# Two transformer blocks on one core: the feed-forward up-projection with high and low activations in one matmul

## The reference

```python
def conv_glu_ffn(h, w_up, conv_w, conv_b, w_down):
    S = h.shape[1]
    u = h @ w_up                       # 256 x 2048 @ 2048 x 11264
    up = jnp.pad(u, ((0, 0), (CONV_WIDTH - 1, 0), (0, 0)))
    u = sum(conv_w[j] * up[:, j:j + S] for j in range(CONV_WIDTH)) + conv_b
    val, gate = jnp.split(u, 2, axis=-1)
    return (jax.nn.silu(gate) * val) @ w_down
```

## Time and profile before

| | |
|---|---|
| median of 3 runs | 2526.63 us (2525.19 to 2527.48) |
| span of the profiled execution | 2525.9 us |
| HBM traffic | 611.66 MB, mean 242 GB/s |
| first up-projection | about 636 to 1124 us of the span |
| second up-projection | about 1760 to 2264 us |
| down-projections | about 1124 to 1370 and 2264 to 2500 us |

### The profile page before, as it was taken

The page is one execution under the profiler, slowest core; times in us unless marked ns, Lnnn a source line. Parts: engine busy times, 40 slices in busy tenths (PEclk is TensorE's granted clock), DMA queues, the critical chain, the costliest instruction groups (busy, mean ns, idle before and its releaser), DMA issues.

```text
span 2525.9 us, 50139 instructions
## 1 busy us (share of the span) xinstructions
PE 2484.3 (98%) x19624; PEld 2273.1 (90%) x19624; DVE 1440.5 (57%) x2436; ACT 1124.3 (45%) x1324; POOL 1232.5 (49%) x500
## 2 busy tenths in 40 slices
PE   7999999999999999999999999999999999999997
PEld 5897998899999999998887877899999999998886
DVE  2536666266767767776665633265766756453433
ACT  2253334434444444454444444344544444454443
POOL 2674445675444444454443666465444444444442
PEclk8999999999999999999999999999999999999998
DMA  9974565596777777777776565386666675556553
GB/s 399 397 271 178 200 234 201 224 385 221 276 286 265 267 274 281 267 260 275 272 272 243 182 258 207 130 313 254 220 233 222 216 258 184 184 180 200 192 191 117
DMA packets 140381, 611.66 MB, mean 242 GB/s; under 512 B 15584, under 2 KB 15968, under 8 KB 115680
## 3 DMA queue, kind: packets, MB, share of 16 engines
q1 hardware_dynamic: 140256, 609.88, 66.4%
HBM read 607.72 MB, written 2.10 MB: 241 GB/s over the span
## 4 chain that ended last, share of the span: by engine, by line
issue 45%; PE 33%; POOL 21%; POOLq 1%; DVE 0%; DMA 0%; ACT 0%; DVEq 0%; SPq 0%
PE psum L1971 33%; POOL wlo L1780 21%; POOLq L1777 0%; DMA ada_raw<-adastream 0%; DVE xT L2314 0%; POOLq L1779 0%; PE psum L2204 0%; DVE psum L2314 0%; ACT arena L1794 0%; POOLq L1780 0%; ACT arena L1791 0%; DVE arena L2429 0%; DVE acc L2306 0%; DVE acc L2314 0%; DVEq L388 0%
## 5 line engine op out<-in xcount | busy, mean ns | idle before, releaser
L1780 POOL TENSOR_TENSOR wlo<-raw,whi 128x1024 fp32r<-128x1024 f32 x496 | 1232.3, 2491 | 1264.2 <-ACT whi L1791 1263.2
L1791 ACT ACTIVATE whi<-raw 128x1024 fp32r<-128x1024 f32 x760 | 800.6, 1058 | 950.1 <-PE psum L1971 716.2
L1971 PE MATMUL psum<-hi_h,whi 128*128 128x256 f32 x4224 | 1206.4, 286 | 4.6 <-DVE lo_h L2314 2.3
L1971 PE MATMUL psum<-lo_h,whi 128*128 128x256 f32 x4224 | 1190.3, 282 | 0.0
L1971 PE MATMUL psum<-hi_h,wlo 128*128 128x256 f32 x4224 | 1190.2, 282 | 0.0
L1971 PEld LDWEIGHTS psum<-hi_h,whi 128*128 128x128 f32 x4224 | 798.4, 189 | 18.7 <-issue 8.5
L1971 PEld LDWEIGHTS psum<-hi_h,wlo 128*128 128x128 f32 x4224 | 798.8, 189 | 1.7 <-issue 1.4
L1971 PEld LDWEIGHTS psum<-lo_h,whi 128*128 128x128 f32 x4224 | 798.4, 189 | 0.0
L2306 DVE TENSOR_TENSOR wlo<-raw,whi 128x1024 fp32r<-128x1024 f32 x264 | 385.1, 1463 | 268.3 <-ACT whi L1791 268.3
L2314 DVE SCALAR_TENSOR_TENSOR psum<-ada_raw,cact,psum 128x256 f32<-128x256 f32 x814 | 342.4, 483 | 24.5 <-DMA ada_raw<-adastream 21.1
L1971 PE MATMUL psum<-whi,gshi 128*128 128x512 f32 x704 | 276.0, 392 | 0.3 <-DVE wlo L2306 0.3
(11 more groups left out here) (166 smaller groups left out, 1608.8 us busy)
## 6 DMA issues: line engine op xcount, KB each, us to landing
raw<-wstream SPq DMA_DIRECT2D x760, 512.0 KB, 4.6
ada_raw<-adastream SPq DMA_DIRECT2D x168, 1024.0 KB, 6.8
arena<-adastream SPq DMA_DIRECT2D x24, 1024.0 KB, 18.0
xT<-x_in SPq DMA_DIRECT2D x8, 512.0 KB, 7.1
y_out<-xT SPq DMA_DIRECT2D x4, 512.0 KB, 2.6
gs_pages<-tabs_in SPq DMA_DIRECT2D x2, 512.0 KB, 4.2
gs_pages<-rw_in SPq DMA_DIRECT2D x2, 512.0 KB, 6.7
tabs<-tabs_in SPq DMA_DIRECT2D x1, 482.0 KB, 8.5
```

Of the source, the lines that this page charges most:

```text
L1780: nc.gpsimd.tensor_tensor(wlo[:, q, :], raw[:, q, :], whi[:, q, :].bitcast(F32), ALU.subtract).then_inc(sem.lo_ready, 1)
L1791: return nc.scalar.activation(out_, in_, ACT.Copy, scale=scale)
L1971: return nc.tensor.matmul(o, lhsT, rhs, start=start, stop=stop, skip_group_check=True)
```

## The change

Where the high weights of a block meet the high and the low activations, the two matmuls of 256 columns become one of 512 columns.

- h is kept in one tensor `h_parts` in which the high and the low part of each row tile lie side by side (512 columns), so that one matmul can read both.
- In the up-projection (`slab_up`) 4 of 4 column tiles of the value half and 2 of 4 of the gate half (`WIDE`) have a PSUM bank each: the left 256 columns take high by high and low weight by high activation, the right 256 columns high weight by low activation. The value half now uses banks 0 to 3, the gate half banks 4 and 5, and its other two tiles share bank 6 with three matmuls as before.
- Behind a half ScalarE copies the right halves of the banks to the arena (`low_taken`), makes the high split of one slab, and waits for `whole`. VectorE, when its running modulation unit is through, waits for `low_taken` and adds the copy to the left halves in PSUM (`whole`). Then the taps follow as before. The high split of slab 11 of a turn comes ahead of the value half's tap (it stood behind it), that of slab 3 of the next turn ahead of the gate half's tap.
- TensorE's first half of an up-projection waits for both older pairs of banks; the first pieces of the down-projection wait for `free_val` alone.
- Some semaphores are shared (`f_exp` with `f_ln`, `gn_var` with `gn_mean`, `conv_landed` with `cols_landed`).

```diff
+WIDE = (4, 2)
-        hi_h, _ = sb("hi_h", [P, KT * S + 128], F32R)
-        lo_h, _ = sb("lo_h", [P, KT * S + 128], F32R)
-        hhi, mhi = (hi_h[:, a:a + KT * S].rearrange("p (k s) -> p k s", s=S) for a in (0, 32))
-        hlo, mlo = (lo_h[:, a:a + KT * S].rearrange("p (k s) -> p k s", s=S) for a in (0, 32))
+        h_parts, _ = sb("h_parts", [P, 2 * KT * S + 128], F32R)
+        hx, mx = (h_parts[:, a:a + 2 * KT * S].rearrange("p (k c s) -> p k c s", c=2, s=S) for a in (0, 32))
+        hhi, mhi = hx[:, :, 0, :], mx[:, :, 0, :]
+        hlo, mlo = hx[:, :, 1, :], mx[:, :, 1, :]
...
+        def up_place(half, j):
+
+            if half == 0 or j < 2:
+                return bank[4 * half + j][:, 0:S]
+            return bank[6][:, (j - 2) * S:(j - 1) * S]
+
+        def up_sums(half, low):
+            b = 4 * half
+            return psum[:, b:b + WIDE[half], low * S:(low + 1) * S]
...
-                        a, z = n1 + half * GS + 3 + (half == 0), n1 + half * GS + 3 + GS
+                        a, z = n1 + half * GS + 4, n1 + half * GS + 3 + GS
...
-                        u = pair(1 - half)
+                        copy(tiles(11 + half)[:, 0:WIDE[half], :], up_sums(half, 1)).then_inc(sem.low_taken, 1)
+                        if i is None:
+                            his(z, z + 1)
+                        else:
+                            hi(z, more, i)
+                        act.wait_ge(sem.whole, 2 * (gb + t + step) + half + 1)
                         for j in range(4):
                             c = 16 * half + 4 * j
-                            ins = fn(tiles(11 + half)[:, j, :], u[:, j, :], ACT.Identity,
+                            ins = fn(tiles(11 + half)[:, j, :], up_place(half, j), ACT.Identity,
                                      scale=cw[:, c:c + 1], bias=cw[:, c + 3:c + 4])
                             if j == 3:
                                 ins.then_inc(sem.gate_tap if half else sem.val_tap, 1)
-                    if i is None:
-                        his(n1 + more + 3, n1 + more + 4)
-                    else:
-                        hi(n1 + more + 3, more, i)
...
+            def slab_up(n, half, k, per=0, i=0):
+
+                ready(n, per, i)
+                q = n % RING
+                first, last = k == 0, k == GS - 1
+                for kk in range(2):
+                    kt = 2 * k + kk
+                    for j in range(4):
+                        w = slice(kk * 512 + j * P, kk * 512 + (j + 1) * P)
+                        if j < WIDE[half]:
+                            b = bank[4 * half + j]
+                            mm(b[:, 0:S], wlo[:, q, w], mhi[:, kt, :], first and kk == 0, False)
+                            ins = mm(b, whi[:, q, w], mx[:, kt, :, :].rearrange("p c s -> p (c s)"), False, last and kk == 1)
+                        else:
+                            ins = product(up_place(half, j), whi[:, q, w], wlo[:, q, w], mhi[:, kt, :], mlo[:, kt, :],
+                                          first and kk == 0 and j % 2 == 0, last and kk == 1)
+                        if kk == 1 and j == 3:
+                            ins.then_inc(sem.slab_used, 1)
...
                             quarter_unit(1, 1)
+                            dve.wait_ge(sem.low_taken, 2 * (NFF * b + done + i) + half + 1)
+                            tt(up_sums(half, 0), up_sums(half, 0), tiles(11 + half)[:, 0:WIDE[half], :],
+                               ALU.add).then_inc(*at.up(sem.whole))
 
                             dve.wait_ge((sem.val_tap, sem.gate_tap)[half], NFF * b + done + 1 + i)
```

More of the change, by code:

```diff
@@ L245, in __init__ @@
         self.sums_taken = new("sums_taken")
+        self.whole = new("whole")
         self.psum_zero = new("psum_zero")
@@ L268, in __init__ @@
         self.f_abs = new("f_abs")
-        self.f_exp = new("f_exp")
         self.f_ln = new("f_ln")
@@ L282, in __init__ @@
         self.gn_sd = new("gn_sd")
-        self.gn_var = new("gn_var")
         self.gs_hi = new("gs_hi")
@@ L305, in __init__ @@
         self.l2v = new("l2v")
+        self.low_taken = new("low_taken")
         self.lo2_ready = new("lo2_ready")
@@ L2155, in body @@
                     for half in range(2):
-                        p = 1 - half
                         free = (sem.free_val, sem.free_gate)[half]
                         if i is None and t == 0:
-                            pe.wait_ge(*st["free"][p])
+                            for p in range(2):
+                                pe.wait_ge(*st["free"][p])
                         else:
@@ L2166, in body @@
                                 pe.wait_ge(sem.h_ready, h0 + k + 1)
-                            slab(n0 + 2 * GS * t + half * GS + k, p, mhi[:, 2 * k:2 * k + 2, :],
-                                 mlo[:, 2 * k:2 * k + 2, :], k == 0, k == GS - 1, 2 * GS * per, 0 if i is None else i)
+                            slab_up(n0 + 2 * GS * t + half * GS + k, half, k, 2 * GS * per, 0 if i is None else i)
                         if units == 2:
@@ L2570, in ffn @@
                                 o, f = (slice(2, S), slice(0, S - 2)) if b == 0 else (slice(0, S - 1), slice(1, S))
-                                stt(t[:, j, o], u[:, j, f], cw[:, c + 2:c + 3], t[:, j, o], ALU.mult, ALU.add).then_inc(*at.up((sem.free_val, sem.free_gate)[half] if j == 3 else sem.step))
+                                stt(t[:, j, o], up_place(half, j)[:, f], cw[:, c + 2:c + 3], t[:, j, o], ALU.mult, ALU.add).then_inc(*at.up((sem.free_val, sem.free_gate)[half] if j == 3 else sem.step))
                         lo2(n1 + 2 * GS + 3, 2 * GS, i)
```

22 lines of the change are left out of this document (11 added, 11 removed).

## The result

The changed kernel takes 2548.3 us (median of 4 runs, 2544.9 to 2551.1) against 2526.5 for the kernel before beside it: a ratio of 1.0085, 95% interval 1.0071 to 1.0098. It is slower by 21.8 us. Forecast were 2516 us and a range of 2505 to 2527, so the time lies outside it, on the other side. The profiled execution took 2548.2 us, its span is 2546.2, 20.3 over the span before.

A forecast was written before the change was run, and what follows sets the result against it. TensorE's matmul issue was taken as the bound (busy 98%). The merge's -22.6 us and the added chain's +12.0 us of stalls, the rest 0, gave -10.6 us: 2516 us, 8-in-10 range 2505 to 2527.

The forecast's parts named there:

- The added chain: At each up-projection half's end, copy and addition of low sums delay the taps; stalls of 12.0 us in all.
- The forecast delay of 1.42: Behind a gate half, SiLU and then GpSimd's split of slab 4 come 1.42 us later; stall about 0.14 us.
- The merge: Up-projection: two 256-column matmuls become one of 512, saving 10.7 ns in each of 2112 pairs, 22.6 us.
- rival 4: Merged up-projection matmul does not save 10.7 ns, chain still stalls: 2531 us; chance 0.07.
- The modulation unit, "0.3 us to spare. Price 0": Unit ends at E' + 22.4, before TensorE's unit sum at 22.7, so no cost.
- Rival 3: GpSimd starts slab 8 before VectorE starts slab 7, unit late, TensorE waits 1.7 us: 2533 us; chance 0.10.
- The moved high split, "it costs nothing": Gate half: slab 3's high split holds ScalarE to 1.72 us, the addition ending at 1.61, so no cost.
- Turns 0 to 7 of block 2: Up-projection turns: value half stalls 0.13 us and gate half 0.57, 0.70 a turn.

The follow-up runs named there:

- e10: Changed kernel without the low sums' copy, addition and their waits, high splits of slabs 11 and 3 back behind ScalarE's tap; 2515.5 us, 0.9952.
- e6: Changed kernel with cw copy at the previous turn's end, low splits of slabs 11 and 3 before the tap's wait, slab 4's high split before SiLU's; 2516.4 us.
- e12: The kernel of e6 with each merged matmul taken apart again into two of 256 columns; 2528.1 us, ratio 1.0004.
- e14: The kernel of e13 with the up-projection's activations starting 64 numbers into their tensor in place of 32; 2524.6 us, ratio 0.9991.
- e8: Kernel before, with only the high splits of slab 11 and of slab 3 of the next turn moved ahead of ScalarE's tap; 2546.5 us, ratio 1.0075.
- e7: Control: kernel before, with VectorE's copy of cw moved from the start of a turn to the end of the one before; 2527.1 us, 1.0002.
- e13: The kernel of e6 with VectorE's low split of slab 5 moved ahead of the small addition modc; 2515.6 us, ratio 0.9957.

## Why the prediction was wrong, step by step

**The added chain: right to a few hundredths.** From the end of a gate half (991.66, the copy less 0.28) the SiLU was forecast at 6.92 and came at 6.92. The forecast delay of 1.42 puts GpSimd's split of slab 4 at 9.01 (7.59 before) and VectorE's of slab 5 at 11.66 (761.84 less 751.60 before); they came at 9.00 and 11.67. Copy, addition of 1024 columns and of 512 measured 1.02, 1.23 and 0.70. In the last turns, which no unit disturbs, the stalls were forecast at 1.14 us and are 1.20 (46.25 against e10's 45.05). That the sums agree so well is in part luck. Forecast were 0.57 in each half; the starts are 0.63 late behind the value half and 0.37 behind the gate half. And a term was missing: behind each of these gaps the second matmul comes 0.1 us late, which makes up for the deadlines that dearer slabs push back.

**The merge: mis-sized by half.** 10.7 ns a pair were taken from matmuls with weights moving; measured are 5.6 (e6 against e12), 11.7 us in place of 22.6. The bounds, 0 and 12.0, held it, but I took a value near one end because it came from a row. The operands were swapped against that row, and rival 4 named this as the reason for doubt, with 0.07. The 2.5 ns that the Trainium skill (TensorE: Matmul & The Clock Gate, Back-to-back issue gap) gives for the fixed part of an isolated matmul lie nearer to the 5.6 than my 10.7 do, and nearer still to the 3 ns that a pair saves in the value halves of block 2 of e14 (356.1 less 353), though the usual distances here lie over its formula, the 118.7 ns by 9.5 and the 226.7 by 10.9. With 11.7 us alone the forecast would have stood at 2526.9, no change.

**The modulation unit, "0.3 us to spare. Price 0": the step that decided the sign.** The prediction followed VectorE by its own delay of 1.42 us, put the order at the port to the test for slabs 7 and 8, and took that of slabs 5 and 6 as it was before. Its own numbers spoke against that: GpSimd was to end slab 4 at 11.64, while slab 6's high part hangs on TensorE and had been there for GpSimd's start 10.41 us behind the half's end in the kernel before (762.01 less 751.60). The pause of 0.19 us that let VectorE through could not outlive a delay of 1.42. The unit's end was tight even as written: 773.75 less 751.60 is 22.15, and with the 0.5 us put on it 22.65, not 22.4, against an E at 22.7. Rival 3 had the mechanism, one pair of slabs too late, and even its end of the unit, 24.4 behind the half's end: measured 1016.07 less 991.66, 24.41, an agreement that is luck, since it comes from another pair. Its stall came out smaller, 0.8 in place of 1.7, because slab 5 now stalls TensorE too (0.6) and the dearer pairs make eight slabs 0.3 us longer. It had a chance of 0.10 and should have had most.

The Trainium skill (SBUF — State Buffer, two separate sides) describes the lock as exclusive for a whole instruction, and each pair above agrees, in either order: 3.42 and 3.47 us for VectorE's split behind GpSimd's, 3.31 and 3.33 for GpSimd's behind VectorE's.

**The moved high split, "it costs nothing": wrong as well.** On its own engine the step was read rightly. What it does is to delay the tap, and with it every later step that hangs on the tap, by 1 us against those that hang on TensorE. Alone it costs 19 us (e8). In the forecast it was hidden behind the copy and the addition, which delay the tap as much. By the forecast's own times (the addition done at 1.61, the split at 1.72) they would have turned the order round without it; no run has the changed kernel with this split back behind the tap, so that is argued and not shown.

**Turns 0 to 7 of block 2: under-sized.** Forecast 0.70 us of stalls, measured 1.42 (46.91 against 45.49). Their gaps are 0.40 and 0.53 behind the gate half and 0.17 behind the value half, each with 0.1 for the next matmul; the second one is slab 5's, the same late split as in block 1, though no unit sum waits there.

**The balance.** Stalls of 1.74 us (47.64, the mean behind the first turn, less 45.90) in ten periods of block 1, of 1.42 in eight and of 1.20 in three make 32.4 us, less 11.7 from the merge 20.7; measured are 20.4 in the two loops. Forecast were 12.0 and 22.6. Of the 31 us between -10.6 and 20.4, 11 belong to the merge and the other 20 to the stalls, above all to those behind the port.

## What to carry to other kernels

Where two engines share a port, write down for each wait what it hangs on: a pause of a few tenths between two operations holds only as long as both sides are delayed together, and a step put into a chain delays one side only. A step moved "into idle time" must be followed to all who hang on its end, not only to its own engine's next deadline. And a price taken from a row with other operands is a bound, not a value; take apart what the change joins in a version with few stalls (as e6 and e12) before building on it.

## What was not expected of the hardware

- A matmul of 512 columns with activations moving costs 230.5 ns from start to start in this kernel, one with weights moving 226.7; in the turn of which a window is shown, the granted clock is 1.00, the level of 2.4 GHz.
- The place where the moving operand begins in SBUF changes that: the last turns take 45.05 us with 128 bytes, 45.33 with 64, 45.44 with 0 and 256 bytes, at equal work.
- VectorE's copy of 32 columns takes 0.17 us by itself and 1.78 in the turn shown, when GpSimd's split is under way (up to 2.03 in that trace), and 0.01 us between two starts decides over 2.2 us of one operation.
- Behind the gaps of TensorE ahead of slabs the second matmul starts 0.1 us late (1006.80 to 1007.02), so a short stall costs 0.1 more than its gap.
- A wait of TensorE of 3.44 us (e8, until 684.70) was followed by 6 us at a granted clock of 0.50, with matmuls 213 ns apart in place of 119. Waits of 1.4 to 1.6 us at the start of block 1 were followed by such a stretch in some executions (e7, e13) and not in others (the kernel before, e6).
